# RWKV's K projection: four of eight weight units in three-part products, two low parts on GpSimd, and R's mixed input computed earlier

## The chip, the cores and the metric

The kernel runs on one core of one Trainium2 chip. The number that counts is the device time of one execution in microseconds (us). Three runs of the kernel before gave 1374.14, 1367.45 and 1371.91, so the median is 1371.91. Everything below about who waits for whom comes from one further, profiled execution of the same kernel.

The engines are named as in the profile: PE is the matrix engine (TensorE), PEld its weight loads, DVE is VectorE, ACT is ScalarE, POOL is GpSimd, and SP is the engine whose queue issues nearly all DMAs (SPq in the rows).

## What is computed

Four layers over 256 tokens of 1024 features: attention with forget gates, a short convolution, RWKV-7 time mixing and differential attention, each followed by an MLP. The change lies in the time mixing. There, cut to what matters:

```
h_prev = h shifted by one token;  hh = h_prev - h
xr = h + hh*mu[0];  xw = h + hh*mu[1];  xk = h + hh*mu[2]
xv = h + hh*mu[3];  xa = h + hh*mu[4];  xg = h + hh*mu[5]
r = xr @ w_r                                  # 1024 x 1024
w = -softplus(-(w0 + tanh(xw @ w1) @ w2)) - 0.5
k = xk @ w_k                                  # 1024 x 1024
v = xv @ w_v
a = sigmoid(a0 + (xa @ a1) @ a2)
kk = k * k_k, normalised by head
```

## The kernel before

All weights pass through one pipeline of units. A unit is 128 rows of a matrix by 1024 columns, 512 KB. SP loads unit i into one of four staging tiles ST (i modulo 4, `load_unit`, L2679). ACT copies it into one of six tiles (i modulo 6). PE multiplies from there.

There are two kinds of units. A **split** unit has a high part SH, rounded to fp32r by ACT, and a low part SL = ST - SH, which DVE computes (`lows`, `low`, L1751 to L1765). Each product is then three fp32r matmuls: high by high, high by low, low by high (`product`, L476). The moving or stationary input needs a high and a low part as well. A **whole** unit is copied by ACT as plain fp32 into the same slot under the name SW, and each product is one fp32 matmul, which the profile records as two passes. SP may overwrite a staging tile of a whole unit when ACT has copied it (semaphore `hi`), and that of a split unit only when its low part is done (`lo`, L2682).

The numbers of the units around the change, used in all that follows: K0 to K7 are the rows of `rw_w_k` (units 213 to 220), R0 and R1 the first rows of `rw_w_r` (221, 222), WA holds the first low-rank matrices of decay and a (`w1`, `a1`, unit 223), R2 and R3 are the next rows of `rw_w_r` (224, 225). Before the change K0 to K7 and WA are whole units. A load of unit i waits for unit i-4 to leave its staging tile: the load of R0 waits for K4, R1 for K5, WA for K6, R2 for K7, R3 for R0.

Every engine's program is written out by hand in a fixed order, and each engine works through its own in order. Around the change:

- **PE** computes K as tokens by columns, in four PSUM banks. It takes K0 to K3 for the first 128 tokens, then for the second, then K4 to K7 for both (L861 to L882). Then R0 to R1 into the same four banks, WA, R2 and R3. Before R0 overwrites a bank pair, PE waits for ACT to have copied K out of it (`kn`).
- **DVE** makes the mixed inputs. `mix_part(g, m)` makes a quarter of K's input XK (half g of the features, token half m): one subtraction HH, a wait for it, then four multiply-adds. `mix(0, XS0)` makes R's input XI and, after ACT has rounded it to XH, its low part XL. `mix_whole(1, XW)` and `mix_whole(4, XA)` make the inputs of decay and of a.
- **ACT** rounds units (`rounded(n)` rounds all up to n-1), copies R's input (`mixed`), and copies K out of PSUM (KN), in the order written at L1519 to L1524.
- **POOL** has small powers for the norms here, then the constants INC and MOD, and a low part of the decay's sigmoid (SGL) later on.

Of the kernel before, what the change touches and what calls it, by code (L numbers as in the profile page):

```python
# [12 lines left out]
S = 256  # L13
# [22 lines left out]
def constant_array():  # L36
# [42 lines left out]
    "conv_dve": "zp c3 zb cl",  # L79
    "inputs_act": "sgh gt kn ts lf sig pp rn gf gg vna mh ht shsq",  # L80
    "inputs_dve": "sgl1 bo ka kk0 mix mixd mixl mixw mk nat ns one rkm tk vnd xg",
}
SHARED = {name: group for group, names in GROUPS.items() for name in names.split()}

class Signals:
# [15 lines left out]
    def inc(self, name, *key):  # L101
        return self.step(name, key, 1)
# [4 lines left out]
    def at(self, name, *key):  # L107
        return self.sem(name), self.table[(name,) + key] if self.nc is not None else 1
# [41 lines left out]
class Units:  # L150
    def __init__(self, A):
# [4 lines left out]
        def rows(w, k, c0=0, c1=D):  # L156
            return w[k * 128:(k + 1) * 128, c0:c1]
# [62 lines left out]
        ple(1)  # L220
        self.stage("rk")
        for k in range(8):
            self.add(rows(A["rw_w_k_2"][0], k), whole=True)
        self.stage("rr")
# [43 lines left out]
    def result(self, at, s, m):  # L268
        return at("used", self.last[s]) if m else at("acc", s)

    def stage(self, name):
# [29 lines left out]
class Memory:  # L301
    def __init__(self, nc):
# [55 lines left out]
        self.HT, self.HH, self.XI = ar("HT", 8, [128, 8, S + 1]), ar("HH", 11, [128, 8, S]), ar("XI", 13, [128, 8, S])  # L358
        self.XK = ar("XK", 9, [128, 8, S])
        self.XV = (ar("XH2", 9, [128, 8, S], F32R), ar("XL2", 10, [128, 8, S], F32R))  # L360
# [35 lines left out]
    def ar(self, name, slot, shape, dt=F32, extra=0):  # L396
        return self.at(name, self.arena + slot * self.slot + extra, shape, dt)
# [54 lines left out]
def tensor_program(e, M, U, sg):  # L452
# [15 lines left out]
    def split(i):  # L468
        w.wait_ge(*at("lo", i))
        return M.SH[i % NSPLIT], M.SL[i % NSPLIT]  # L470
# [382 lines left out]
    def plain(i, x, k, m, banks, start, stop):  # L853
        ws = whole(i)
        for n in range(2):
            t = mm(bank(banks[2 * m + n]), x[:, k, tokens(m)], ws[:, n * 512:n * 512 + 512], start, stop)
        return t
# [18 lines left out]
    for m in range(2):  # L876
        w.wait_ge(*at("mk", 1, m))
    for k in range(4, 8):
        t = plain(uk + k, M.XK, k, 0, (0, 1, 2, 3), False, k == 7)
        if k == 7:  # L880
            t.then_inc(*inc("acc", "rk"))
        plain(uk + k, M.XK, k, 1, (0, 1, 2, 3), False, k == 7).then_inc(*inc("used", uk + k))  # L882

# [401 lines left out]
def scalar_program(e, M, U, sg):  # L1285
# [12 lines left out]
    def rounded(n):  # L1298
        for i in range(done[0], n):
            round_unit(i)  # L1300
        done[0] = n
# [216 lines left out]

    rounded(224)  # L1519
    mixed(0, XH0)  # L1520
# [211 lines left out]
def vector_program(e, M, U, sg):  # L1732
# [18 lines left out]
    def lows(n):  # L1751
        for i in range(done[0], n):
            if i not in U.whole:
                low(i)
        done[0] = n
# [360 lines left out]

    KN, KK, RN, AG, TT = M.KN, M.KK, M.RN, M.AG, M.TT
    lows(223)
    mix_whole(1, M.XW)
    mix(0, M.XS[0])  # L2120
    lows(225)
    mix_whole(4, M.XA)
# [332 lines left out]
def gpsimd_program(e, M, U, sg):  # L2455
# [83 lines left out]


    e.tensor_copy(M.INC[:, :], CC[:, C_SUI + 128:C_SUI + 256])
    tt(M.MOD[:, :].rearrange("p (r n) -> p r n", r=4), CC[:, C_I64:C_I64 + 32].unsqueeze(1).to_broadcast([128, 4, 32]),
# [121 lines left out]
def sync_program(e, M, U, sg, A, out):  # L2664
# [14 lines left out]
    def load_unit(i):  # L2679
        t, x = M.ST[i % NSTAGE], U.src[i]  # L2680
        if i >= NSTAGE:
            w.wait_ge(*at("hi" if i - NSTAGE in U.whole else "lo", i - NSTAGE))  # L2682
        for p0, p1, c0, c1, src in x if isinstance(x, list) else [(0, 128, 0, U.cols[i], x)]:
            o = t[p0:p1, c0:c1]
            if len(src.shape) == 3:
                o = o.rearrange("p (k n) -> p k n", k=src.shape[1])
            load(f"load{i % NSTAGE}", (i,), o, src)
# [155 lines left out]
```

## Time and profile before

| | us |
|---|---|
| median of three runs | 1371.91 |
| profiled execution | 1370.58 |
| its span, first to last instruction | 1368.8 |
| PE busy | 1340.3 (98%) |
| DVE busy | 862.4 (63%) |
| ACT busy | 724.6 (53%) |
| POOL busy | 187.4 (14%) |

The span lies 1.8 us under the time of its own execution, and that execution 1.3 us under the median. The granted clock of TensorE is 1.00, the upper of its two levels (2.4 GHz), over the whole stretch that is spoken of here. Times in rows count from the first instruction of the span. A row's first number is its start, the second what it took, and "[0.66 <-PE PS L459]" says how long its engine sat idle before it and which instruction ended that.

### The profile page before, as it was taken

The page shows a single profiled execution, that of the slowest core. Times are in us where ns is not written, and L with a number is a line of the kernel's source. Part 1 is how long each engine was busy: PE and PEld are TensorE (multiplying, and loading weights), DVE is VectorE, ACT ScalarE, POOL GpSimd, SP SyncE. Part 2 cuts the span into 40 slices and gives each one's busy share as a digit, 9 for nine tenths or more (in the row PEclk, how much of TensorE's full clock was granted, in tenths as well). Part 3 has the DMA queues.
Part 4 walks back from the last instruction along what each step waited for, and adds up shares of the span by engine and source line. Part 5 has one row for each costly group of instructions (what it writes and reads, how often), then busy time and mean ns, then how long its engine had stood idle before and what let it go on. Part 6 is the DMA issues. An engine that isn't in the chain of part 4 may idle for free.

```text
span 1368.8 us, 24119 instructions
## 1 busy us (share of the span) xinstructions
PE 1340.3 (98%) x10262; PEld 1144.7 (84%) x10262; DVE 862.4 (63%) x1199; ACT 724.6 (53%) x1028; POOL 187.4 (14%) x179
## 2 busy tenths in 40 slices
PE   8999999999999999999999998999999999999999
PEld 8976989988898889988466877899998877799998
DVE  5657754557667655456798668655555678665554
ACT  5456654446654654445566554554454667654452
POOL 0263011000000011010131356000000134000000
PEclk9999999999999999999999999999999999999999
DMA  8634554665564555664547301555474532655472
GB/s 307 215 114 153 194 192 164 214 200 169 160 225 168 180 195 167 221 197 158 177 127 219 84 19 49 173 181 185 147 251 157 197 127 78 191 179 185 147 253 78
DMA packets 91519, 232.54 MB, mean 170 GB/s; under 512 B 20614, under 2 KB 26646, under 8 KB 91290
## 3 DMA queue, kind: packets, MB, share of 16 engines
q1 hardware_dynamic: 90840, 228.95, 51.7%
q0 software_dynamic: 576, 2.11, 0.5%
q8 instruction: 76, 1.25, 0.4%
q14 instruction: 27, 0.22, 0.1%
HBM read 227.87 MB, written 1.08 MB: 167 GB/s over the span
## 4 chain that ended last, share of the span: by engine, by line
PE 85%; DVE 6%; ACT 4%; DMA 2%; issue 1%; POOL 1%; SPq 1%; DVEq 0%; ACTq 0%; POOLq 0%
PE PS L459 82%; PE PS L462 4%; ACT SH L1296 1%; DVE SL L1746 1%; DMA ST<-in_w_attn_in 1%; DMA ST<-in_rw_w_v 1%; DVE XX L1740 1%; ACT JK L1293 1%; SPq L2672 1%; DVE SL L1740 1%; ACT AB L1293 0%; DVE X L1746 0%; POOL SM L2461 0%; DVE XL L1740 0%; ACT XT L1296 0%
## 5 line engine op out<-in xcount | busy, mean ns | idle before, releaser
L1746 DVE SCALAR_TENSOR_TENSOR SL<-ST,SM,SH 128x1024 fp32r<-128x1024 f32 (+1 forms) x256 | 315.5, 1255 | 155.1 <-ACT SH L1296 153.7
L1296 ACT ACTIVATE SH<-ST,SM 128x1024 fp32r<-128x1024 f32 (+1 forms) x256 | 281.7, 1121 | 177.1 <-PE PS L459 110.7
L459 PE MATMUL PS<-XH,SH 128*128 128x256 f32 x1224 | 343.6, 282 | 0.1
L459 PE MATMUL PS<-XH,SL 128*128 128x256 f32 x1224 | 343.2, 281 | 0.0
L459 PE MATMUL PS<-XL,SH 128*128 128x256 f32 x1224 | 342.3, 281 | 0.0
L1740 DVE TENSOR_TENSOR SL<-ST,SH 128x1024 fp32r<-128x1024 f32 (+1 forms) x153 | 192.9, 1276 | 142.4 <-ACT SH L1296 142.1
L1296 ACT ACTIVATE SH<-ST 128x1024 fp32r<-128x1024 f32 (+1 forms) x153 | 158.6, 1052 | 153.7 <-PE PS L459 124.6
L459 PEld LDWEIGHTS PS<-XH,SH 128*128 128x128 f32 x1224 | 231.4, 190 | 1.7 <-issue 0.7
L459 PEld LDWEIGHTS PS<-XL,SH 128*128 128x128 f32 x1224 | 228.6, 187 | 0.9
L459 PEld LDWEIGHTS PS<-XH,SL 128*128 128x128 f32 x1224 | 228.7, 187 | 0.2
L459 PE MATMUL PS<-SH,XH 128*128 128x512 f32 x544 | 220.8, 406 | 3.2 <-DVE SL L1740 1.6
L459 PE MATMUL PS<-SL,XH 128*128 128x512 f32 x544 | 214.1, 394 | 0.0
L459 PE MATMUL PS<-SH,XL 128*128 128x512 f32 x544 | 211.7, 394 | 1.7 <-DVE XL L1740 1.7
L459 PE MATMUL PS<-SH,HXH 128*128 128x512 f32 (+1 forms) x436 | 171.8, 394 | 0.9 <-DVE HXL L1740 0.9
L459 PE MATMUL PS<-SH,HXL 128*128 128x512 f32 (+1 forms) x436 | 170.2, 390 | 0.0
L459 PE MATMUL PS<-SL,HXH 128*128 128x512 f32 (+1 forms) x436 | 169.9, 390 | 0.0
L459 PEld LDWEIGHTS PS<-SH,XH 128*128 128x128 f32 x544 | 102.1, 188 | 33.8 <-issue 5.9
L2461 POOL TENSOR_TENSOR SM<-SM 128x2 f32<-128x2 f32 (+3 forms) x41 | 46.9, 1147 | 592.6 <-DVE SM L1743 540.7
L459 PEld LDWEIGHTS PS<-SH,XL 128*128 128x128 f32 x544 | 101.9, 188 | 26.6 <-DVE XL L1740 2.4
L459 PEld LDWEIGHTS PS<-SL,XH 128*128 128x128 f32 x544 | 102.4, 188 | 20.9
L459 PEld LDWEIGHTS PS<-SH,HXL 128*128 128x128 f32 x436 | 81.9, 188 | 19.4
L459 PEld LDWEIGHTS PS<-SH,HXH 128*128 128x128 f32 x436 | 81.8, 188 | 19.1 <-DVE HXL L1740 1.8
(262 smaller groups left out, 1380.3 us busy)
## 6 DMA issues: line engine op xcount, KB each, us to landing
ST<-in_ffn_w_gu SPq DMA_DIRECT2D x80, 512.0 KB, 4.9
ST<-in_w_mlp_up SPq DMA_DIRECT2D x64, 512.0 KB, 5.2
ST<-in_w_mlp_down SPq DMA_DIRECT2D x64, 512.0 KB, 4.4
ST<-in_ffn_w_down SPq DMA_DIRECT2D x44, 512.0 KB, 4.4
ST<-in_w_attn_in SPq DMA_DIRECT2D x24, 512.0 KB, 5.0
ST<-in_w_conv_in SPq DMA_DIRECT2D x24, 512.0 KB, 4.5
ST<-in_w_ple_gate SPq DMA_DIRECT2D x16, 512.0 KB, 3.6
ST<-in_kv_w SPq DMA_DIRECT2D x16, 512.0 KB, 3.5
```

Of the source, the lines that this page charges most:

```text
L459: return e.matmul(o, l, r, start=start, stop=stop, skip_group_check=True)
L462: return e.transpose(o, x, ID)
L1293: return e.activation(o, x, f, **kw)
L1296: return e.activation(o, x, ACT.Copy, **kw)
L1740: return e.tensor_tensor(o, x, y, op)
L1746: return e.scalar_tensor_tensor(o, x, a, y, op, op2)
L2461: return e.tensor_tensor(o, x, y, op)
L2672: e.dma_start(o, x, allow_slow_non_contiguous=slow).then_inc(*dma(name, *key))
```

## The change

K4 to K7 become split units, so their products are three fp32r matmuls each. For that, the half of XK that they use gets a rounded copy (ACT, new tile XKS, blocks 0 to 3) and a rest (DVE, XKS, blocks 4 to 7), token half by token half. The low parts of K4 and K5 are computed by POOL (`pool_low`, semaphore `lop`) and those of K6 and K7 by DVE. On DVE, `mix(0)` moves ahead of `mix_whole(1)` and also ahead of the low parts of R0 and R1. The low part of R2 moves behind `mix_whole(4)`.

```diff
         self.stage("rk")
+        self.pool_low = {len(self.src) + 4, len(self.src) + 5}
         for k in range(8):
-            self.add(rows(A["rw_w_k_2"][0], k), whole=True)
+            self.add(rows(A["rw_w_k_2"][0], k), whole=k < 4)
...
+    def low_part(self, at, i):
+        return at("lop" if i in self.pool_low else "lo", i)
...
     for m in range(2):
-        w.wait_ge(*at("mk", 1, m))
-    for k in range(4, 8):
-        t = plain(uk + k, M.XK, k, 0, (0, 1, 2, 3), False, k == 7)
-        if k == 7:
-            t.then_inc(*inc("acc", "rk"))
-        plain(uk + k, M.XK, k, 1, (0, 1, 2, 3), False, k == 7).then_inc(*inc("used", uk + k))
+        w.wait_ge(*at("xkl", m))
+    columns("rk", range(uk + 4, uk + 8), (M.XKS[:, 0:4, :], M.XKS[:, 4:8, :]), range(4), (0, 1, 2, 3), False, True)
...
-    rounded(224)
+    for m in range(2):
+        rounded(219 + m)
+        w.wait_ge(*at("mk", 1, m))
+        copy(M.XKS[:, 0:4, tokens(m)], M.XK[:, 4:8, tokens(m)]).then_inc(*inc("xkh", m))
+    rounded(223)
     mixed(0, XH0)
     rounded(226)
...
-            if i not in U.whole:
+            if i not in U.whole and i not in U.pool_low:
                 low(i)
...
+    for m in range(2):
+        w.wait_ge(*at("xkh", m))
+        rest(M.XKS[:, 4:8, tokens(m)], M.XK[:, 4:8, tokens(m)], M.XKS[:, 0:4, tokens(m)]).then_inc(*inc("xkl", m))
+    lows(221)
+    mix(0, M.XS[0])
     lows(223)
     mix_whole(1, M.XW)
-    mix(0, M.XS[0])
-    lows(225)
     mix_whole(4, M.XA)
     lows(226)
...
+    for i in sorted(U.pool_low):
+        w.wait_ge(*at("hi", i))
+        tt(M.SL[i % NSPLIT][:, :], M.ST[i % NSTAGE][:, :], M.SH[i % NSPLIT][:, :].bitcast(F32), ALU.subtract).then_inc(*inc("lop", i))
     e.tensor_copy(M.INC[:, :], CC[:, C_SUI + 128:C_SUI + 256])
...
-            w.wait_ge(*at("hi" if i - NSTAGE in U.whole else "lo", i - NSTAGE))
+            w.wait_ge(*(at("hi", i - NSTAGE) if i - NSTAGE in U.whole else U.low_part(at, i - NSTAGE)))
```

How the instructions of DVE stand from the last quarter of XK to the first use of K, before the change (SL_66 and SL_61 are the low parts of R0 and R1, SL_63 and SL_64 those of R2 and R3):

```order
L1740 TENSOR_TENSOR HH<-HT 128x4x128
L1746 SCALAR_TENSOR_TENSOR XK<-HH,SM,HT 128x128 x4
L1740 TENSOR_TENSOR SL_66<-ST_68,SH_54 128x1024
L1740 TENSOR_TENSOR SL_61<-ST_69,SH_49 128x1024
L1746 SCALAR_TENSOR_TENSOR XW<-HH,SM,HT 128x256 x8
L1746 SCALAR_TENSOR_TENSOR XI<-HH,SM,HT 128x256 x8
L1740 TENSOR_TENSOR XL_82<-XI,XH_81 128x1024 x2
L1740 TENSOR_TENSOR SL_63<-ST_67,SH_51 128x1024
L1746 SCALAR_TENSOR_TENSOR XA<-HH,SM,HT 128x256 x8
L1740 TENSOR_TENSOR SL_64<-ST_68,SH_52 128x1024
L1740 TENSOR_TENSOR KK<-KN,PR_72 128x1024 x2
```

The same stretch of DVE in the changed kernel (the first SL_64 and SL_65 are the low parts of K6 and K7):

```order
L1746 TENSOR_TENSOR HH<-HT 128x4x128
L1752 SCALAR_TENSOR_TENSOR XK<-HH,SM,HT 128x128 x4
L1746 TENSOR_TENSOR XKS<-XK,XKS 128x4x128 x2
L1746 TENSOR_TENSOR SL_64<-ST_70,SH_52 128x1024
L1746 TENSOR_TENSOR SL_65<-ST_67,SH_53 128x1024
L1752 SCALAR_TENSOR_TENSOR XI<-HH,SM,HT 128x256 x8
L1746 TENSOR_TENSOR XL_82<-XI,XH_81 128x1024 x2
L1746 TENSOR_TENSOR SL_66<-ST_68,SH_54 128x1024
L1746 TENSOR_TENSOR SL_61<-ST_69,SH_49 128x1024
L1752 SCALAR_TENSOR_TENSOR XW<-HH,SM,HT 128x256 x8
L1752 SCALAR_TENSOR_TENSOR XA<-HH,SM,HT 128x256 x8
L1746 TENSOR_TENSOR SL_63<-ST_67,SH_51 128x1024
```

The low part of R0 stood directly behind XK. Now two rests, two low parts, the eight operations of XI and the two of XL are ahead of it.

ACT between the copies of the shifted input HT and those of K (KN), before the change (SW_56 first is K4, then K5, K6, K7 to SW_59, R0 SH_54, R1 SH_49, WA SW_56, R2 SH_51, R3 SH_52):

```order
L1296 ACTIVATE HT<-PS 128x4x128 x2
L1296 ACTIVATE SW_56<-ST_68 128x1024
L1296 ACTIVATE SW_57<-ST_69 128x1024
L1296 ACTIVATE SW_58<-ST_70 128x1024
L1296 ACTIVATE SW_59<-ST_67 128x1024
L1296 ACTIVATE SH_54<-ST_68 128x1024
L1296 ACTIVATE SH_49<-ST_69 128x1024
L1296 ACTIVATE SW_56<-ST_70 128x1024
L1296 ACTIVATE XH_81<-XI 128x1024 x2
L1296 ACTIVATE SH_51<-ST_67 128x1024
L1296 ACTIVATE SH_52<-ST_68 128x1024
L1296 ACTIVATE KN<-PS 128x1024 x2
```

The same stretch of ACT in the changed kernel, from K4 (SH_50) on:

```order
L1297 ACTIVATE SH_50<-ST_68 128x1024
L1297 ACTIVATE SH_51<-ST_69 128x1024
L1297 ACTIVATE XKS<-XK 128x4x128
L1297 ACTIVATE SH_52<-ST_70 128x1024
L1297 ACTIVATE XKS<-XK 128x4x128
L1297 ACTIVATE SH_53<-ST_67 128x1024
L1297 ACTIVATE SH_54<-ST_68 128x1024
L1297 ACTIVATE SH_49<-ST_69 128x1024
L1297 ACTIVATE XH_81<-XI 128x1024 x2
L1297 ACTIVATE SW_56<-ST_70 128x1024
L1297 ACTIVATE SH_51<-ST_67 128x1024
L1297 ACTIVATE SH_52<-ST_68 128x1024
```

Two copies of XK stand between K5, K6 and K7, and WA is copied after XH. In both orders the copies KN come directly behind SH_52, that is behind R3.

## Rows read from the trace of the kernel before

**Rows 1.** The page: busy times, and the chain that ended last by engine.

```profile
PE 1340.3 (98%) x10262; PEld 1144.7 (84%) x10262; DVE 862.4 (63%) x1199; ACT 724.6 (53%) x1028; POOL 187.4 (14%) x179
...
PE 85%; DVE 6%; ACT 4%; DMA 2%; issue 1%; POOL 1%; SPq 1%; DVEq 0%; ACTq 0%; POOLq 0%
```

**Rows 2.** The chain in order of time, 656 to 760: start, us, what.

```profile
656.89 57.60 PE PS L459 x220
...
726.94 10.32 DMA ST<-in_rw_w_v
```

**Rows 3.** Windows: busy us of each engine, clock, DMA share and GB/s.

```profile
672.70:686.30 13.60, 13.60 (x34) 5.93 (x32) 13.11 (x25) 7.15 (x7) 0.00 (x0) 1.00 0.46 134
```

**Rows 4.** Timeline of PE, K's second part to R1: start, us, what.

```profile
663.96 22.73 PE L459 MATMUL PS<-SW,XK 128*128 128x512 f32 x52
686.29 0.63 PE L459 MATMUL PS<-SH,XH 128*128 128x512 f32 x1
...
689.30 0.40 PE L459 MATMUL PS<-SH,XH 128*128 128x512 f32 x1
...
691.86 0.39 PE L459 MATMUL PS<-SH,XL 128*128 128x512 f32 x1
```

**Rows 5.** Timeline of DVE, 665 to 684.

```profile
665.68 0.69 DVE L1740 TENSOR_TENSOR HH<-HT 128x512 f32<-128x512 f32 x1
666.40 1.14 DVE L1746 SCALAR_TENSOR_TENSOR XK<-HH,SM,HT 128x128 f32<-128x128 f32 x4
...
668.18 1.14 DVE L1746 SCALAR_TENSOR_TENSOR XK<-HH,SM,HT 128x128 f32<-128x128 f32 x4
672.43 1.23 DVE L1740 TENSOR_TENSOR SL<-ST,SH 128x1024 fp32r<-128x1024 f32 x1 [3.10 <-ACT SH L1296]
...
675.29 3.25 DVE L1746 SCALAR_TENSOR_TENSOR XW<-HH,SM,HT 128x256 f32<-128x256 f32 x8
...
681.62 2.43 DVE L1740 TENSOR_TENSOR XL<-XI,XH 128x1024 fp32r<-128x1024 f32 x2
```

**Rows 6.** Timeline of ACT, 664 to 688.

```profile
664.16 0.60 ACT L1296 ACTIVATE HT<-PS 128x512 f32<-128x512 f32 x1 [0.29 <-PE PS L459]
664.66 1.99 ACT L1296 ACTIVATE SW<-ST 128x1024 f32<-128x1024 f32 x2
...
673.05 1.06 ACT L1296 ACTIVATE SH<-ST 128x1024 fp32r<-128x1024 f32 x1 [0.66 <-PE PS L459]
...
682.70 1.99 ACT L1296 ACTIVATE SH<-ST 128x1024 fp32r<-128x1024 f32 x2
685.01 1.02 ACT L1296 ACTIVATE KN<-PS 128x1024 f32<-128x1024 f32 x1 [0.32 <-PE PS L459]
```

**Rows 7.** Timeline of POOL: an HXL of layer one, then 660 to 715.

```profile
185.38 2.41 POOL L2461 TENSOR_TENSOR HXL<-HU,HXH 128x1024 fp32r<-128x1024 f32 x1 [0.85 <-ACT HXH L1296]
...
661.91 0.45 POOL L2461 TENSOR_TENSOR MOD<-CC 128x128 f32<-128x128 f32 x1
...
707.70 4.83 POOL L2461 TENSOR_TENSOR SGL<-SGR,SGH 128x1024 fp32r<-128x1024 f32 x1 [8.55 <-ACT SGH L1296]
```

**Rows 8.** Timeline of DVE beside those two POOL operations.

```profile
186.29 4.86 DVE L1740 TENSOR_TENSOR SL<-ST,SH 128x1024 fp32r<-128x1024 f32 x3 [2.08 <-ACT SH L1296]
...
705.89 3.25 DVE L1746 SCALAR_TENSOR_TENSOR XI<-HH,SM,HT 128x256 f32<-128x256 f32 x8
709.06 4.55 DVE L1740 TENSOR_TENSOR XL<-XI,XH 128x1024 fp32r<-128x1024 f32 x2
```

**Rows 9.** Timeline of ACT, the rounding that the second XL waits for.

```profile
709.17 1.06 ACT L1296 ACTIVATE XH<-XI 128x1024 fp32r<-128x1024 f32 x1 [0.53 <-DVE XI L1746]
```

**Rows 10.** Tile XL on DVE, 640 to 760: duration ns min/median/max.

```profile
L1740 DVE TENSOR_TENSOR XL<-XI,XH x4: 1214/1222/3349, 681.6 to 710.3; 128x1024 fp32r<-128x1024 f32 x4
```

**Rows 11.** Loads of R's units: count, KB, median us to landing; 661 to 676, then 676 to 690.

```profile
ST<-in_rw_w_r SPq DMA_DIRECT2D x4, 512.0 KB, 4.6
...
ST<-in_rw_w_r SPq DMA_DIRECT2D x2, 512.0 KB, 3.5
```

More of the change, by code:

```diff
@@ L79 @@
     "conv_dve": "zp c3 zb cl",
-    "inputs_act": "sgh gt kn ts lf sig pp rn gf gg vna mh ht shsq",
-    "inputs_dve": "sgl1 bo ka kk0 mix mixd mixl mixw mk nat ns one rkm tk vnd xg",
+    "inputs_act": "sgh gt kn ts lf sig pp rn gf gg vna mh ht shsq xkh",
+    "inputs_dve": "sgl1 bo ka kk0 mix mixd mixl mixw mk nat ns one rkm tk vnd xg xkl",
 }
@@ L358, in __init__ @@
         self.HT, self.HH, self.XI = ar("HT", 8, [128, 8, S + 1]), ar("HH", 11, [128, 8, S]), ar("XI", 13, [128, 8, S])
-        self.XK = ar("XK", 9, [128, 8, S])
+        self.XK, self.XKS = ar("XK", 9, [128, 8, S]), ar("XKS", 10, [128, 8, S], F32R)
         self.XV = (ar("XH2", 9, [128, 8, S], F32R), ar("XL2", 10, [128, 8, S], F32R))
@@ L468, in split @@
     def split(i):
-        w.wait_ge(*at("lo", i))
+        w.wait_ge(*U.low_part(at, i))
         return M.SH[i % NSPLIT], M.SL[i % NSPLIT]
```

## The prediction

> **What bounds the kernel now.** I read the page first: PE is busy 98% of the span and makes up 85% of the chain that ended last [rows 1]. So a microsecond counts only if it moves PE. The chain in order of time comes next. From 656.89 it is PE alone for 57.6 us, so K, R and the low-rank products follow each other without a stop, and what comes later (the exponentials of the decay, then loads of `rw_w_v` queued behind a copy of them) hangs on PE's end there [rows 2]. A shift of PE at 690 is therefore handed down in full: those loads are issued after ScalarE's result, not by a clock of their own. In the window in which K4 to K7 are multiplied PE is busy 13.60 of 13.60 us, at a granted clock of 1.00, while DVE is busy 13.11 of 13.60 [rows 3]. The reader should keep that second number: DVE has half a microsecond to spare there, and the change gives it more to do.
>
> **PE's saving.** K4 to K7 are 4 units x 2 token halves x 2 column halves = 16 products. As fp32 they are 32 recorded passes in 13.6 us [rows 3], 0.43 us a pass; 52 passes in 22.73 us say the same [rows 4]. As split products they are 48 matmuls. In R1 twelve such matmuls start from 689.30 to 691.86, eleven steps of 0.233 us [rows 4], so 48 take 11.2 us. That is 2.4 us less. The switch from fp32 to fp32r (0.47 us to the second matmul at 686.29 in place of 0.23 [rows 4]) only moves from R0 to K4. This is the whole gain that the change can bring. The reordering of mixes brings PE nothing of its own, since before R0 PE waited for no mixed input.
>
> **When K4 may start.** Before, PE came to K4 at 672.7; DVE's last quarter of XK had been ready since 668.18 + 1.14 = 669.3 [rows 5]. Now the quarter is rounded by ACT (0.60 us for 128x512, as HT [rows 6]) and its rest taken by DVE (0.7 us, as HH [rows 5]), which gives 670.6, still 2.1 us early. What decides is POOL. Its queue is empty after 662.4 [rows 7], and ACT has copied K4 at 665.7 and K5 at 666.65 [rows 6], so both of POOL's subtractions are waiting while DVE is at XK.
>
> What such an operation costs is in the trace. Alone it takes 2.41 us for 128x1024 [rows 7]. The twelve HXL of the first blocks come in six pairs, and at each pair the second meets DVE's low parts. At the first of them POOL holds from 185.38 to 187.79, and the three SL that start at 186.29 take 4.86 us instead of about 3.5 [rows 7, 8]. The nearest case is SGL. POOL issues at 707.70, in the middle of eight XI, and ends at 712.53: 4.83 us, twice its price. One of DVE's two XL took 3.35 us instead of 1.22 [rows 8, 10]. POOL did not get in between the XI, which follow each other without a wait. It got in at 710.1, where the second XL waited for ACT's rounding until 709.17 + 1.06 = 710.23 [rows 9], and then DVE stood still for 2.1 us. I take from this: the two exclude each other when both read their inputs from SBUF, and POOL enters at any point where DVE pauses for a semaphore, even for less than a tenth of a microsecond.
>
> The Trainium skill ("SBUF — State Buffer", Who interferes with whom) states this as an exclusive lock: a DVE instruction with two SBUF inputs and a GpSimd instruction that reads SBUF block each other for a whole instruction, and whoever starts first wins. By that rule, this trace agrees (3.35 against 1.22 us). Without it the sum would be that of the first rival.
>
> Between HH and its XK DVE has such a pause (666.37 to 666.40 [rows 5]), since XK waits for HH. So: POOL takes K4 from 666.4 to 668.8. The third quarter of XK ends at 669.9 instead of 667.5, the next HH at 670.6. There POOL takes K5, to 673.0. The last quarter of XK ends at 674.1 instead of 669.3. ACT's copy 674.7, DVE's rest 675.4. PE starts K4 at 675.4, 2.7 us late, and ends K at 675.4 + 11.2 = 686.6, against 686.3. The saving is already gone.
>
> **When R0 may start.** This is the step that I expect to decide. PE may overwrite K's banks only after ACT's copies KN, and in ACT's order KN stands behind the rounding of R3. R3's load waits for the low part of R0 to leave its staging tile. Before, that low part was DVE's first work after XK (672.43 [rows 5]), so R3 lay ready, and ACT rounded R2 and R3 at 682.70 and copied K at 685.01, 0.3 us after PE had it [rows 6]. Now the low part of R0 is computed after mix(0). From 675.4, with 1.2 us for a low part or an XL and 3.2 us for eight multiply-adds [rows 5]:
> - low parts of K6 and K7, to 677.8; XI, to 681.0.
> - XH on ACT is in time: R1's load can go out when POOL has K5 done (673.0), lands 4.6 us later [rows 11] and is rounded by 678.7; the first half of XI is there at 679.4.
> - two XL, to 683.4; low part of R0, to 684.6.
> - R3's load: 3.5 us to landing when little else is under way, 4.6 us when much is [rows 11]. By 684 the loads of WA and R2 have landed, so I take 3.5: 688.1.
> - rounding of R3, half of 1.99 [rows 6], to 689.1; KN for the first tokens 1.02 [rows 6], to 690.1.
>
> PE starts R0 at 690.2 instead of 686.29 [rows 4]. The second token half finds its KN ready by then. Sum: +3.8 us, with the slow landing +4.9.
>
> **What else moves.** XW and XA now end at about 684.6 + 1.2 + 6.4 = 692.2. PE needs them after R0 and R1, at 690.2 + 5.6 = 695.8, so they have 3.6 us of cover; without that shift of R0 they would be late themselves. SP's queue holds the load of R3 behind those of WA and R2, which are out by 678.6, so it adds nothing. ACT's extra copies (1.2 us) and the later WA (after XH) lie in its waits. INC and MOD on POOL come 11 us later than at 661.9 [rows 7] and are needed only for the decay's sums after 713. All later steps of this stage start from R0, so they keep their distances.
>
> Against its own execution: 1370.6 + 3.8 = 1374.4 us. The profiled run lies 1.3 us under the median of the runs shown, so on that footing 1371.9 + 3.8 = 1375.7; I say 1375.5. That is 0.27% more, under the 0.5% (7 us) that a measurement of this kernel can tell from no change.
>
> **The rivals.**
> - *POOL and DVE don't hold each other up here* (POOL done with K4 at 668.2, K5 at 670.6). For it: XK is four short operations with a scalar from SBUF, and all that was seen to block were long ones; POOL might also slip in where it costs less. Against it: the row of SGL and six of HXL. Then K4 starts at 672.7 and K ends at 683.9. R1's load lands at 675.3, its rounding ends at 676.4, XH at 677.5 and 678.5, XL at 679.8, the low part of R0 at 681.0, R3 lands at 684.5 to 685.6, KN is there at 686.5 to 687.6. R0 starts 0 to 1.2 us later than before: about 1372.5. The saving is still lost, now in the second step alone.
> - *The gain comes through*: nothing after K waits, and R0 starts 2.4 us earlier, 1369.5. It would need R3 to land by 681.9, before its load has even gone out by any sum above. Only an error of mine in who waits for whom would allow it.
> - *Slower by more than 0.5%.* POOL misses the short pauses of HH and XK and enters only where DVE waits for ACT. Then K4's low part runs from 670.0 to 672.4 (the rest of the second half waits), and the next real pause is after XI, at 678.7, where DVE waits for XH. K5's low part ends at 681.1. R1's load waits for it, and ACT rounds R1 before XH: landing 684.6, rounding 685.7, XH 687.8, XL 689.1, low part of R0 690.3, R3 lands 693.8, KN 695.8. R0 starts 9.5 us late: 1381.4. It decides from the point where POOL's second operation isn't begun by 674. Against it: SGL got in at a pause of under 0.1 us [rows 8, 9].
>
> **Chances.** Forecast 0.64, no blocking 0.15, gain 0.05, POOL starved 0.12, anything else 0.04. The forecast's own numbers run from 1375.5 to 1376.7 by the landing; the three runs before spread over 7 us, so a median of another day may lie 2 us off. 1369.8 to 1380 takes in the forecast and the first rival with that, and leaves out the starved case and half of the gain. Faster by over 0.5% is under 1365, below every case: 0.02. Slower by over 0.5% is over 1378.8: the starved case and the upper tail of the forecast, 0.14. The rest, 0.84, is within 0.5%.
>
> **What would show it.** In the profile of the changed kernel: the two POOL subtractions about 2.4 and 4 us long, back to back from 665.8 to about 673; two of the XK quarters at 3.5 us instead of 1.14; K4 starting near 675.4 with PE idle about 2.7 us before it, released by the rest XKS; 48 matmuls in 11.2 us; R3's rounding starting only when its load has landed, near 688; PE idle 3 to 4 us before R0, released by KN; XW and XA after that with no wait of PE on them. If PE runs from K3 to K4 without a gap, the blocking is wrong; if KN is copied right after K's last product, the second step is wrong, and the time would be at or below that of before. A low clock anywhere in this stage would be something I have not priced.

## The result, and the profile after

| | before | after |
|---|---|---|
| median | 1371.8 us (16 runs, 1367.45 to 1374.14) | 1375.08 us (16 runs, 1372.96 to 1379.64) |
| profiled execution | 1370.58 us, mean clock 1.000 | 1378.1 us, mean clock 0.996 |

The ratio is 1.0032, 95% interval 1.0023 to 1.0040: the changed kernel is 0.23 to 0.40% slower, 3.2 to 5.5 us. The two medians lie 3.3 us apart. The prediction said 1375.5. Much of what follows is about why that number is better than its reasons.

The page of after, busy times and the chain that ended last:

```profile
PE 1341.9 (97%) x10278; PEld 1151.2 (84%) x10278; DVE 870.3 (63%) x1203; ACT 725.6 (53%) x1030; POOL 192.7 (14%) x181
PE 83%; DVE 8%; ACT 4%; DMA 2%; issue 2%; POOL 1%; SPq 0%; ACTq 0%; DVEq 0%; POOLq 0%
```

PE issues 16 matmuls more (10278 against 10262 [rows 1]). Keep that count, it comes back. PE's share of the chain fell from 85% to 83%, and DVE has 8% of it. The chain of waits of after, start and length in us, shows where (pieces called "issue", under 0.3 us each, are left out). Before, there was one piece here, 57.60 us of PE [rows 2]:

```profile
665.07 0.61 ACT HT L1297
...
668.21 5.43 DVE XK L1752 x4
...
674.27 1.15 DVE XK L1752 x4
675.45 0.64 ACT XKS L1297
676.11 0.69 DVE XKS L1746
676.80 2.27 DVE SL L1746 x2
679.08 3.17 DVE XI L1752 x8
682.25 2.35 DVE XL L1746 x2
684.60 1.14 DVE SL L1746
685.76 3.54 DMA ST<-in_rw_w_r
689.32 1.06 ACT SH L1297
690.38 0.92 ACT KN L1297
...
691.55 28.07 PE PS L464 x140
```

Read it from the bottom up: R0 (691.55) waits for KN, KN stands behind the rounding SH of R3, that for R3's load, the load for the low part SL of R0, and that for DVE, which has been late since a quarter of XK took 5.43 us. PE does not appear between 665 and 691.5, so nothing that it saves there counts.

One correction must be made before times are compared. In the profiled execution of after TensorE's clock was at half rate for 3.4 us from 28.6 us on, in a part of the program that both kernels share. All of after is 1.8 us late from there to this stage (the second HT of this stage starts at 665.97 and before at 664.16 [rows 6]). "Corrected" below means less that amount; for other kernels the amount is their own.

DVE and POOL of after in the same stretch (start, length, count, and in brackets the idle time before and what ended it). The rows that end in x1 are single operations out of the merged ones:

```profile
667.49 0.68 DVE L1746 TENSOR_TENSOR HH<-HT 128x512 f32<-128x512 f32 x1
668.21 5.43 DVE L1752 SCALAR_TENSOR_TENSOR XK<-HH,SM,HT 128x128 f32<-128x128 f32 x4
...
674.27 1.14 DVE L1752 SCALAR_TENSOR_TENSOR XK<-HH,SM,HT 128x128 f32<-128x128 f32 x4
...
667.59 5.15 POOL L2470 TENSOR_TENSOR SL<-ST,SH 128x1024 fp32r<-128x1024 f32 x2 [4.08 <-ACT SH L1297]
...
667.59 2.80 POOL L2470 TENSOR_TENSOR SL<-ST,SH 128x1024 fp32r<-128x1024 f32 x1 [4.08 <-ACT SH L1297]
...
668.21 2.32 DVE L1752 SCALAR_TENSOR_TENSOR XK<-HH,SM,HT 128x128 f32<-128x128 f32 x1
...
670.34 2.39 POOL L2470 TENSOR_TENSOR SL<-ST,SH 128x1024 fp32r<-128x1024 f32 x1
...
670.45 2.43 DVE L1752 SCALAR_TENSOR_TENSOR XK<-HH,SM,HT 128x128 f32<-128x128 f32 x1
```

POOL's two low parts run back to back, and DVE's four multiply-adds that overlap them take 5.43 us instead of 1.14. The single rows say how. POOL's first operation is recorded from 667.59, while DVE is still at HH (0.68 us, its usual length), so it got through at DVE's pause from 668.17 to 668.21. The first multiply-add, recorded from 668.21, ends 0.14 us after that operation of POOL does. Then POOL's second operation holds up the second multiply-add, and the last two are short again. Between those two multiply-adds DVE waits for no semaphore. PE at the two places where it now stops:

```profile
676.91 0.54 PE L464 MATMUL PS<-SH,XKS 128*128 128x512 f32 x1 [2.15 <-DVE XKS L1746]
...
691.55 0.47 PE L464 MATMUL PS<-SH,XH 128*128 128x512 f32 x1 [1.66 <-ACT KN L1297]
```

Corrected, K4 starts at 675.1 and R0 at 689.8, where before it started at 686.29 [rows 4]: 3.5 us late. After the first of these stops the granted clock fell, which the prediction had not priced. Windows of after (busy time of PE, PEld, DVE, ACT, POOL, then the granted clock, DMA share, GB/s):

```profile
676.90:680.30 3.40, 3.39 (x9) 2.64 (x10) 3.40 (x6) 2.03 (x3) 0.00 (x0) 0.54 0.37 84
691.55:694.95 3.40, 3.40 (x15) 2.78 (x16) 3.40 (x7) 0.66 (x1) 0.00 (x0) 1.00 0.29 65
```

A mean of 0.54 says that nearly all of this window was at 1.2 GHz. It cost K about 1.7 us (9 matmuls where there is room for about 15), but K's end is not on the path: R0 would have waited for KN anyway.

Behind R0 two more things differ. The chain reaches a load of `w_v` that took 10.32 us before [rows 2] and takes 8.87 us after (from 732.21), so 1.45 us of the delay is absorbed there, and from 741 to 768 after is only 2.0 us late (corrected). Then, in the stage of the heads, PE stops at a place where before did not:

```profile
775.84 1.44 PE L464 MATMUL PS<-Z,XT 64*64 64x64 f32 x59
...
778.99 0.34 PE L464 MATMUL PS<-Z,XT 64*64 64x64 f32 x5 [1.72 <-issue]
779.53 1.97 PE L467 MATMUL PS<-CC,XX 128*128 128x128 f32 x8 [0.20 <-issue]
```

"issue" means that nothing the profile shows was waited for. These 64 products run without a break before the change. The stop takes 1.9 us, the clock falls right after it (779.6), and by 859 us after has become 3.7 us later than it was at 768. So the profiled 7.5 us are 1.8 (clock at 28.6) + 2.0 (K and R0) + 3.7 (heads, of which the low clock is 1.7). This execution is 3.0 us above the median of after, so not all of it is typical.

Stops of this kind are not new. The kernel before has them in the same stage, at other matmuls, and these two are 128 matmuls apart:

```profile
793.02 0.27 PE L459 MATMUL PS<-VN,KN 64*64 64x64 f32 x2 [1.01 <-issue]
...
796.48 0.39 PE L459 MATMUL PS<-VN,KN 64*64 64x64 f32 x10 [0.80 <-issue]
```

### The profile page after: what moved, and what is told of

Its sections match the earlier page's. It is cut to its first block, busy times and chain, and to the rows that moved or that the text cites. A ratio compares the mean times of both kernels' runs of the same rounds, so it can differ in the third digit from the quotient of the medians.

```text
span 1376.3 us, 24159 instructions
## 1 busy us (share of the span) xinstructions
PE 1341.9 (97%) x10278; PEld 1151.2 (84%) x10278; DVE 870.3 (63%) x1203; ACT 725.6 (53%) x1030; POOL 192.7 (14%) x181
## 4 chain that ended last, share of the span: by engine, by line
PE 83%; DVE 8%; ACT 4%; DMA 2%; issue 2%; POOL 1%; SPq 0%; ACTq 0%; DVEq 0%; POOLq 0%
PE PS L464 79%; PE PS L467 4%; DVE SL L1752 1%; ACT SH L1297 1%; DMA ST<-in_w_attn_in 1%; DVE SL L1746 1%; DVE XK L1752 1%; DMA ST<-in_rw_w_v 1%; DVE XL L1746 1%; ACT AB L1294 0%; DVE XX L1746 0%; DVE X L1752 0%; POOL SM L2470 0%; DMA ST<-in_w_mlp_up 0%; ACT JK L1294 0%
## 5 line engine op out<-in xcount | busy, mean ns | idle before, releaser
L1297 ACT ACTIVATE SH<-ST 128x1024 fp32r<-128x1024 f32 (+1 forms) x157 | 162.6, 1052 | 154.6 <-PE PS L464 119.9
```

What stands on the lines that cost most here:

```text
L1297: return e.activation(o, x, ACT.Copy, **kw)
```

## The experiments

The theory after the first comparison: R0 is late by the chain above, and that sets the time. Rivals: DVE's new order alone (with R's mix first), POOL alone, or something outside this stage. All kernels were timed in 5 rounds beside the kernel before (median 1370.57, 1369.99 and 1370.22 us in the three groups).

**KN first.** ACT copies K before it rounds R3.

```diff
-    rounded(226)
+    rounded(225)
     for m in range(2):
         w.wait_ge(*U.result(at, "rk", m))
         copy(M.KN[:, m, :], ...)
+    rounded(226)
```

> The changed kernel, with ACT copying K out of PSUM (KN) ahead of the rounding of R3 instead of behind it. Theory (two steps: POOL and DVE exclude each other and delay K4; then R0 waits for KN, which stands behind R3's load): the second wait goes, R0 starts when K ends, 1.6 us earlier than in the changed kernel's profile, so about 1373.5 against 1375.1. K4 stays as late as it was. Rival (the order on ACT is harmless, all of the loss is K4's late start and the half clock behind it): no idle PE before R0 either way and the time stays at 1375.1.

1374.72 us (12 runs), ratio 1.0026 (1.0012 to 1.0040), where 1373.5 was expected; the time does not tell it from after. The wait before R0 is gone: R0 follows K's last product. But K itself ends late, by the wait before K4 (2.15 us) and the low clock behind it, so R0 still starts 1.7 us late (689.98, corrected 688.0). Once KN no longer holds R0, the wait before K4 and the low clock behind it are on the path.

**POOL's low parts given back to DVE.**

```diff
-        self.pool_low = {len(self.src) + 4, len(self.src) + 5}
+        self.pool_low = set()
```

> The changed kernel, with DVE instead of POOL computing the low parts of K4 and K5. Theory: XK is no longer stretched (1.14 us a quarter), K4 starts without a gap after K3, at full clock, and K ends 4 us earlier than in the changed kernel; but low R0 and R3's load come only about 1 us earlier, so R0 still starts 2 to 3 us later than before the change, with PE idle 4 to 5 us before it, long enough that the granted clock may fall: about 1374, 1375 if the clock falls. Rival (the loss is only POOL's): faster than before the change, about 1369.5.

1376.18 us (11 runs), ratio 1.0037 (1.0025 to 1.0049), the slowest of this group, and slower than the 1374 to 1375 expected. PE runs through K without a stop and then waits three times as long:

```profile
690.49 0.77 PE L464 MATMUL PS<-SH,XH 128*128 128x512 f32 x1 [5.21 <-ACT KN L1297]
```

So POOL and DVE's exclusion is not what makes R0 late. DVE has 2.3 us of low parts more in place of 4.3 us of standing still, the chain through R3's load is nearly as long, and R0 is 3.1 us late (corrected) instead of 3.5. After the 5.21 us of idling the clock was at half rate from 688.1 to 694.9, this time on R0's path.

**Low parts of R0 and R1 ahead of the mix.** DVE's program:

```diff
-    lows(221)
-    mix(0, M.XS[0])
     lows(223)
+    mix(0, M.XS[0])
     mix_whole(1, M.XW)
```

> The changed kernel, with DVE computing the low parts of R0 and R1 ahead of R's mixed input, as before the change. Theory: R3's load goes out 5 us earlier and KN is copied right behind K's last product, so R0 starts 1.6 us earlier than in the changed kernel, K4 as late as there: about 1373.5. The mixed input ends 5 us after K4's start plus what it waits, still ahead of K's end. Rival (moving R's mixed input ahead helps and undoing it costs): slower than 1375.1, PE waiting for XL before R0.

1374.36 us (12 runs), ratio 1.0026 (1.0013 to 1.0039), where 1373.5 was expected. Again R0 starts as soon as K ends, and again K ends late. Further down PE stands still for 1.7 us before the sums of the sigmoid (719.21), where after does not. That this comes from R's input being later on DVE is not shown. Each of the first three undoes one link; none wins the time back.

**All three at once.** No POOL low parts, KN first (both as above), and in DVE's `mix`, between XI and XL:

```diff
             t.then_inc(*inc("mix", i, g))
+        lows(223)
```

> The changed kernel with three edits: no low part on POOL, KN ahead of R3's rounding, and the low parts of R0 and R1 between XI and XL. Theory: nothing waits between K3 and R0, K4 to K7 take 11.2 us instead of 13.6, R0 starts 2.2 us earlier than before the change: about 1369.6, less than both kernels. Rival (the split's extra work on ACT and DVE, 6 us of DVE in a stretch where it had half a microsecond free, costs as much again in a later wait, of PE on XA before WA or on R2's low part): 1372 or more.

1373.03 us (12 runs), ratio 1.0018 (1.0006 to 1.0030): the rival's time, not the 1369.6 of the theory. R0 starts 2.2 us earlier than before (corrected), which is nearly the 2.4 us that the split products save. So the gain is real and can be let through. It is lost further on:

```profile
714.84 0.47 PE L464 MATMUL PS<-SGH,INC 128*128 128x512 f32 x1 [2.75 <-issue]
...
776.37 0.34 PE L464 MATMUL PS<-Z,XT 64*64 64x64 f32 x5 [1.45 <-issue]
```

The first is a wait for ACT's sigmoid behind XH behind DVE, which is never idle from 665 to 715 us: four more low parts and two rests have used up what it had to spare. The second is the stop in the heads again.

**The new order without the split.** The kernel before, DVE's program:

```diff
+    mix(0, M.XS[0])
     lows(223)
     mix_whole(1, M.XW)
-    mix(0, M.XS[0])
-    lows(225)
     mix_whole(4, M.XA)
```

> The kernel before, with only DVE's order changed: R's mixed input ahead of the low parts of R0 and R1 and of the decay's input. K stays whole. Theory (R3's load hangs on R0's low part, and KN on R3's rounding): K4 starts and K ends as before, R3's load goes out 8 us later, near 682, and R0 starts 1 to 2 us late, with PE idle for it. Part of that is given back at the loads of w_v: 1371 to 1372. Rival (the order is harmless by itself): 1370.6 and R0 at 686.3.

1372.30 us (11 runs), ratio 1.0014 (1.0004 to 1.0024). The chain through R3's load appears with K still fp32:

```profile
686.97 1.06 ACT L1296 ACTIVATE SH<-ST 128x1024 fp32r<-128x1024 f32 x1 [4.52 <-DMA ST<-in_rw_w_r]
...
689.19 0.47 PE L459 MATMUL PS<-SH,XH 128*128 128x512 f32 x1 [1.03 <-ACT KN L1296]
```

R0 is 1.4 us late (689.19 less the 1.5 us by which this profiled execution is late ahead of this stage, against 686.29). The order alone makes the second step; with the split and POOL ahead of it, it becomes 3.5.

**Half of POOL's work.** POOL's two low parts, those of K4 and K5 (the expectation names K6 and K7 by mistake), cover 512 of 1024 columns, and the kernel leaves out the rest of them:

```diff
-        tt(M.SL[i % NSPLIT][:, :], M.ST[i % NSTAGE][:, :], ...
+        tt(M.SL[i % NSPLIT][:, 0:512], M.ST[i % NSTAGE][:, 0:512], ...
```

> The changed kernel with GpSimd's two low parts cut to 512 of their 1024 columns: the other half of the low parts of K6 and K7 is left out, so this run says nothing of K's values. A dose test of the exclusion. Theory: GpSimd holds VectorE off for as long as it works, so the stretched quarter of XK takes about 1.1 + 2.2 = 3.3 us instead of 5.43, XKS and with it K4 come 2.1 us earlier, the wait before K4 (2.15 us) goes to 0 to 0.3 and TensorE's clock stays at full rate there; the low part of R0 and R3's load come 2.1 us earlier too, so R0 is 1.3 to 1.6 us late instead of 3.5. The stop before Z,XT stays, since TensorE's program is as long. Median about 1.5 us below the changed kernel: 1373.5 (1372.3 to 1374.5). Rival (the quarter is long for another reason, as the order of the mixes): the quarter stays above 5 us and the time at 1375.

The stage came out as written, in the first two lines below; the time did not: 1376.55 us (5 runs), ratio 1.0044 (1.0029 to 1.0059), where 1373.5 was expected. That would be a ratio of 1.0024, below this interval, so the gain did not come. Whether the kernel is slower than after stays open, since their intervals overlap.

```profile
667.35 3.27 DVE L1752 SCALAR_TENSOR_TENSOR XK<-HH,SM,HT 128x128 f32<-128x128 f32 x4
...
666.73 2.99 POOL L2470 TENSOR_TENSOR SL<-ST,SH 128x512 fp32r<-128x512 f32 x2 [4.08 <-ACT SH L1297]
...
688.49 0.77 PE L464 MATMUL PS<-SH,XH 128*128 128x512 f32 x1 [3.15 <-ACT KN L1297]
```

POOL 5.15 to 2.99 us, DVE's quarter 5.43 to 3.27: the same 2.16 us less on both. That is the exclusion measured by dose. Here too two of the four multiply-adds are long (1.24 and 1.35 us). K4 no longer waits, K ends 3.7 us earlier than in after, and R0 is 1.3 us late as forecast (corrected 687.6). But PE now has its whole idle time in one piece of 3.15 us before R0, and the clock falls there:

```profile
688.49:691.89 3.40, 3.40 (x8) 2.75 (x9) 3.40 (x7) 0.66 (x1) 0.00 (x0) 0.50 0.41 90
...
687.30:694.10 6.80, 5.61 (x13) 4.51 (x14) 6.80 (x12) 2.32 (x4) 0.00 (x0) 0.50 0.61 166
```

8 matmuls in the first 3.4 us where after has 15 in the window from its R0, and the second line shows that the half rate lasted twice as long as in after, 6.8 us. 5.6 us of that lie on R0's path, which costs about 2.8 us of work.

**Keeping TensorE busy before K4.** After, with two products on constants (four matmuls in the profile) ahead of the wait for XKS:

```diff
+    busy(2, 6)
     for m in range(2):
         w.wait_ge(*at("xkl", m))
```

> The changed kernel, with two matmuls of 512 columns into an unused bank on PE just before it waits for K4's input (XKS). They fill 1.7 of the 2.15 us in which it stood idle and after which the granted clock was 0.54 for 3.4 us. Theory: the clock stays at 1.00, K ends 1.7 us earlier, and nothing comes of it, since R0 waits for KN behind R3's load: PE's idle time before R0 grows from 1.7 to about 3.4 us, time 1375.1 (with a risk that the clock falls there instead). Rival (the low clock is what costs): 1373.4.

1377.81 us (5 runs), ratio 1.0048 (1.0034 to 1.0061). K4's wait shrinks to 0.42 us, the clock holds at 1.00 through K, and then:

```profile
689.73 0.77 PE L464 MATMUL PS<-SH,XH 128*128 128x512 f32 x1 [3.26 <-ACT KN L1298]
```

R0 starts at the same time as in after (corrected), with a low clock on its path that after does not have:

```profile
688.90:695.60 6.70, 5.88 (x14) 4.65 (x15) 6.70 (x11) 2.30 (x3) 0.00 (x0) 0.50 0.50 148
```

The price of the low clock in after was hidden behind R0's wait. Filling the first wait made the second one longer, and about 2.9 us of work (half of the 5.88 busy) were lost where nothing hides them. The expectation had this as its risk. The stop in the heads stands four matmuls earlier than in after, as many as were added:

```profile
780.01 0.35 PE L464 MATMUL PS<-Z,XT 64*64 64x64 f32 x9 [1.53 <-issue]
```

Here, as in e6_half_pool and e2_no_pool, a wait of over 3 us before R0 was followed by 6.8 us at half rate, and the wait of 1.66 us in after by none. In between, the length alone does not decide: the clock fell after 2.15 us in after and 2.47 us in e10_gates_pad32, and stayed at 1.00 after 2.75 us in e5_all_three and 2.54 us in e9_gates_first (its run is below).

**Padding alone.** Nothing of the change: the kernel before, with the two products of 512 columns on constants before K0 replaced by ten of 32 columns. They are 16 matmuls more in the profile, exactly after's 10278, and K0 starts 0.1 us later by them.

```diff
-    busy(2, 0)
+    busy(10, 0, width=32)
```

> The kernel before, with two idle-filling matmuls of 512 columns on PE (ahead of K, in a stretch where PE waits for ScalarE anyway) replaced by ten of 32 columns. That adds to PE's program about as many instructions as the change does, and nothing else. In the profiles of all five changed kernels so far PE stands still for 1.2 to 1.7 us near 777, with no releaser (issue), at the same matmul Z,XT of the heads' stage, where the kernel before has no such stop. Theory A (the stop comes from where the instructions lie, which a longer program shifts): the stop appears here too, and the time is 1 to 2 us over the kernel before, 1371.6 to 1372.6. Theory B (it comes from what DVE, POOL or DMA do in the changed kernels): no stop, 1370.6.

1372.84 us (11 runs), ratio 1.0018 (1.0008 to 1.0028): by the ratio 2.5 us for nothing that any engine waits for. And the stop in the heads is there, at the same matmul:

```profile
773.55 1.44 PE L459 MATMUL PS<-Z,XT 64*64 64x64 f32 x59
775.88 0.34 PE L459 MATMUL PS<-Z,XT 64*64 64x64 f32 x5 [0.90 <-issue]
```

But this stop is not seen to make the kernel slower. Over the stretch of the heads, from the first product on tile T to the one that waits for TC (764.13 to 842.56 before, 765.64 to 843.75 here), TensorE takes 78.4 us before and 78.1 us here: the kernel before has stops of 1.01, 0.80, 1.37 and 0.80 us in that stretch, and here they are 0.41, 0.90, 0.84 and 0.41 us, beside the new one. The profiled execution is 1.0 us longer than that of before, and 1.8 us of lateness come from a low clock at 28.5 us, far ahead of the padding. So what the 2.5 us of the median consist of stays open.

**A better order on the same base.** All three at once, and ACT takes the second half's sigmoid (`gates_of(1)`) ahead of V's rounded input, and DVE its rest ahead of V's. ACT's part, of all three at once:

```diff
+    gates_of(1)
     for g in range(2):
         mixed_half(3, M.XV[0], g)
-    gates_of(1)
```

> The kernel e5_all_three, in whose profile R0 started 2.2 us earlier than before but PE then stood still for 3.2 us before the sums of the decay, waiting for a sigmoid of ACT that stands behind the rounding of V's mixed input, which DVE makes late. Here ACT computes the second half's sigmoids before it rounds V's input, and DVE the rest of the decay's sigmoid before that of V's input. Theory (DVE has no idle time left between 667 and 717, and the sigmoid merely stood in its queue): the wait goes, PE stays about 2 us ahead up to the exponentials, and the time is 1 to 2 us under e5_all_three, 1371 to 1372, near the kernel before. Rival (DVE's extra work comes out elsewhere): no change from 1373.0.

1372.12 us (11 runs), ratio 1.0013 (1.0001 to 1.0026). Its profiled execution, 1367.75 us with the clock at 1.00 throughout and R0 at 683.89, is the fastest of its eleven runs, so it flatters the kernel. The stop is at the same place:

```profile
772.45 0.33 PE L464 MATMUL PS<-Z,XT 64*64 64x64 f32 x5 [0.90 <-issue]
```

**The same, with 16 matmuls of padding more.** The edit of the padding above, in e9_gates_first.

> e9_gates_first with 8 more short products on constants (32 more TensorE instructions) ahead of K, in the same place as in e8_pad_before. Tells whether the stop before Z,XT in the heads' stage hangs on where TensorE's instructions lie. Theory A (placement): the stop of 0.9 us moves to another instruction, and the time moves with it, either way, by 1 to 2 us: 1370.5 to 1374. Theory B (the stop belongs to what the heads' stage waits for, whatever the length of the program): the stop stays before the same five products, and the time stays at 1372.1 within 0.6.

1370.62 us (11 runs), ratio 1.0002 (0.9993 to 1.0011). The median is 1.5 us below that of e9_gates_first, but the two were timed in different groups and their intervals overlap, so a gain is not shown. In the profiles the stretch of the heads is longer here, 79.1 us against 78.0. The stop has moved:

```profile
771.33 0.45 PE L464 MATMUL PS<-Z,XT 64*64 64x64 f32 x12 [0.44 <-issue]
...
776.42 0.57 PE L464 MATMUL PS<-Z,XT 64*64 64x64 f32 x21 [1.58 <-issue]
```

This version has the lowest median with split K. It can't be told from the kernel before. In both, PE still waits before the `XG` products for ACT's PP, 2.5 us, where before waited 0.8.

**Twice the padding in the kernel before.** `busy(18, 0, width=32)`.

> The kernel before with 16 more short products on constants (64 more TensorE instructions) ahead of K, twice the pad of e8_pad_before. Theory A (where TensorE's instructions lie decides where it stops for them): the stops of the heads' stage stand elsewhere than in the kernel before and in e8_pad_before, one or two of them where nothing hides them: 1371.5 to 1374. Theory B (the 2.5 us of e8_pad_before were the padding's own time or the wait's): the padding of twice the length costs twice as much, 1375. Rival C (e8_pad_before's was chance): 1370.3.

1374.64 us (12 runs), ratio 1.0027 (1.0017 to 1.0036). Inconclusive as to the time. The eighteen short products were far dearer than I had reckoned: K0 starts 2.85 us late, and the clock falls at 658.3, so 1374.64 is mostly the padding's own price, as the expectation's theory B had it. For the place of the stop it is clear:

```profile
774.71 0.45 PE L459 MATMUL PS<-Z,XT 64*64 64x64 f32 x11 [0.18 <-issue]
...
779.53 0.57 PE L459 MATMUL PS<-Z,XT 64*64 64x64 f32 x21 [1.32 <-issue]
```

**Four times the padding in e9_gates_first.** `busy(34, 0, width=32)`.

> e9_gates_first with 32 more short products on constants (128 more TensorE instructions) ahead of K. The products themselves take about 0.06 us each, 2 us in all, of which what TensorE waits there for K's first mixed input hides a part, so K may start 0 to 1.5 us later. Theory A (placement): the stops of the heads' stage stand elsewhere again; if they fall where TensorE is not the bound, 1370.5, else up to 1374. Theory B (length adds nothing but its own time): 1372.1 to 1373.6, the stop before the same products as in e9_gates_first.

1379.77 us (6 runs), ratio 1.0064 (1.0050 to 1.0078): a miss. K0 starts at 666.32 instead of 656.69: the padding's 68 recorded matmuls took 11.24 us where the four longer ones had taken 1.88, and not the 2 us that I had worked out. The total tells nothing of placement, but the profile does: the `Z,XT` products run without a stop, and the stretch of the heads takes 76.4 us, the least of all the kernels here.

What the profiles say of the stop, taken together. With 10262 matmuls in PE's program (before, e4_order_alone) there is none in the `Z,XT` products. With 10278 (after, e1 to e3, e5, e6, e8, e9) it stands before the last 5 of the same 64, whatever the order on the other engines, with K split or not. With 10282 (e7_busy) it stands before the last 9, and with 10294 (e10, e11) before the last 21: one matmul earlier for each one added ahead of it. So where it appears, its place is a fixed position in PE's program. Whether it appears is another matter: by the same count it would stand 11 matmuls behind that block in before and e4_order_alone, and inside another block in e12_gates_pad128 (10342 matmuls), and none of the three shows it. That it is the fetching of instructions is likely (the page of the profile counts 77 packets of kind "instruction" on queue q8 in every kernel of 10278 matmuls and more, 76 in before and e4_order_alone), but no run measured the fetch itself. And the place is all that is shown: how much time the kernel takes does not follow from this one stop.

## Why the prediction was near, and where it was wrong

*PE's saving, 2.4 us: right.* K's 48 matmuls take 0.233 us each at full clock, and in e5_all_three R0 starts 2.2 us earlier than before.

*POOL and DVE exclude each other: right in effect, wrong in detail.* I had POOL take one operation at each of two pauses, with two quarters of XK at 3.5 us, 4.8 us of delay in all. It got in at the first pause (668.2), its second operation ran right behind the first, and one quarter took 5.43. The delay is 4.3 us, and K4 at 675.1 is where 675.4 was forecast. My rule that POOL enters only where DVE pauses for a semaphore does not hold: the second operation held up a multiply-add in the middle of a group. The first rival (no blocking) is dead, by e6_half_pool's dose. The starved rival is dead too: POOL was in at a pause under 0.1 us long.

*R0 behind KN behind R3's load: right.* 3.5 us late against 3.8. R3's load took 3.54 us, as chosen. The order alone gives 1.4 us of it.

*XW and XA have cover: right.* No PE wait on them in after.

*"All later steps of this stage start from R0, so they keep their distances": wrong.* At 768 only 2.0 of the 3.5 us are left; 1.45 of the rest went into the load of `w_v`, which took 8.87 us instead of 10.32. I had argued that those loads have no clock of their own. Their issue hangs on PE; the time that they take does not.

*What the sum left out: the rest of the time.* With 2.0 us in place of 3.8 the forecast would have been 1373.7. The measured 3.3 (by the ratio 4.4) needs another 1.3 to 2.4, and the sum has no term for it. What the runs show is more low clock. The mean granted clock over all runs was 0.9972 in after, and 0.9994 to 0.9996 in the kernel before's runs of the three groups. In a span of this length one stretch of 3.4 us at half clock takes 0.00125 off that mean. My estimate from these numbers: 0.0023 of 1376 us are 3.2 us of TensorE's work, the stretch behind K4's wait (1.7 us) is hidden, so 1.5 us are not, and 2.0 + 1.5 is 3.5. This is worked out from means and shown by no run. Padding alone gives 2.5 us by the ratio, with a mean clock of 0.9987; about 1.2 us of that would be low clock by the same estimate. So two errors, 1.8 us too much for the chain and nothing for what TensorE loses elsewhere, cancelled. The step that I would have to defend did not hold by itself, and the number did: its nearness is luck.

*The low clock "that I have not priced".* It fell after K4's wait, at a price of 1.7 us, all of it hidden under R0's wait. In e1_kn_first, where that wait is gone, it is on the path, and in e6_half_pool and e7_busy the longer wait before R0 brought one of 6.8 us there.

What stays open: why the stop costs 0.90 us in some kernels and up to 1.72 in others at the same instruction, why it is absent in e12_gates_pad128, why the clock falls more often in the kernels with more matmuls, and what padding's 2.5 us consist of.

## What to carry to other kernels

When an engine on the path is made faster, look for the buffer that its consumer must first empty, and follow that consumer's queue back to the loads: here the gain of 2.4 us was in the kernel all the time, behind a copy that stood in line after a rounding that waited for a load. Moving idle time of TensorE together into one piece before a critical product can bring a low clock onto the path (about 2.8 us of work after a wait of 3.15 us), so judge an edit that removes a hidden wait by the wait that is left. And before a difference of 0.1 to 0.3% is put down to an order of work, pad the kernel before to the same number of instructions and time that: here the pad alone gave 2.5 us by the ratio, and the change 4.4. And when a stop turns up in a new place, add up all stops of the stage in both kernels before giving it the blame.

## What the runs showed of the hardware that I had not expected

- A pause of DVE of 0.04 us let POOL in, and POOL's two operations (5.15 us) ran one right behind the other, although DVE had multiply-adds to do that waited for no semaphore. One of those ended 0.14 us after POOL's first operation, the next took 2.43 us instead of 0.35.
- TensorE's granted clock was at half rate for 3.4 us after an idle time of 2.15 us (after) and for 6.8 us after 3.15 (e6_half_pool), 3.26 (e7_busy) and 5.21 (e2_no_pool). It stayed at 1.00 after 1.66 us in after, but also after 2.54 (e9_gates_first) and 2.75 (e5_all_three). The work lost was about half of the busy time in such a stretch: 1.7 us in after, 2.8 in e6_half_pool.
- TensorE makes stops of 0.4 to 1.9 us that no semaphore ends, in every kernel here. 16 matmuls more ahead of them moved one by exactly 16 matmuls. The length of PE's program alone, 16 matmuls in 10262, changed the median by 2.5 us (by the ratio), but in the profiles the stretch with the stops was no longer for it (78.1 us against 78.4).
- Matmuls of 32 fp32 columns are not nearly free: the 20 recorded ones took 2.32 us in e8_pad_before (0.12 us each), 68 took 11.24 us in e12_gates_pad128 (0.17, most of it at half clock), and there, as with 36 of them in e11_before_pad64, the clock fell while TensorE was doing nothing else (at 658.9 and 658.3).
